# When two column sums, one output tile and one layer's side work are placed later in a slot stream

## The reference

```python
for i in range(DEPTH):                       # DEPTH = 4, kinds 0, 1, 2, 0
    xn = rms_norm(h, norm_gain[i])
    m = diff_attention(...) | mla(...) | rglru_block(...)      # kind = i % 3
    h = h + m
    g = sigmoid(rms_norm(h, ple_norm[i]) @ ple_w_gate[i])
    h = h + g * (p[i] @ ple_w_proj[i])
```

## Time and profile before

| | |
|---|---|
| median of 3 runs | 3595.81 us (3591.43 to 3596.21) |
| the profiled execution | 3592.54 us, its span 3590.7 us |
| TensorE busy | 3481.8 us, 97% of the span |
| VectorE, ScalarE, GpSimd busy | 77%, 55%, 16% |
| mean granted TensorE clock | 0.991 |

### The profile page before, as it was taken

How to read it: one execution, slowest core, us unless ns; L and a number is a source line. 1 busy time by engine, 2 the same in 40 slices (tenths; PEclk the granted TensorE clock), 3 DMA queues, 4 the chain that set the end, 5 groups by cost and what they waited for, 6 DMA issues and landing times.

```text
span 3590.7 us, 68527 instructions
## 1 busy us (share of the span) xinstructions
PE 3481.8 (97%) x27986; PEld 3404.9 (95%) x27986; DVE 2782.3 (77%) x4529; ACT 1981.2 (55%) x3204; POOL 560.6 (16%) x546
## 2 busy tenths in 40 slices
PE   7999999999999999999999999999999999999997
PEld 7999999999999999999999999999999998999997
DVE  7787788677797887877877797888888867666665
ACT  6554546656556686565554446665656646434344
POOL 2111112111113011131111112221212310000000
PEclk9999999999999999999999999999999999999999
DMA  6555556544465444655555475445454444555552
GB/s 240 208 196 214 206 203 240 183 161 167 155 270 193 175 165 176 264 187 211 204 214 200 172 280 186 156 165 212 165 211 165 155 163 148 191 208 183 216 188 106
DMA packets 104905, 691.17 MB, mean 192 GB/s; under 512 B 12688, under 2 KB 21008, under 8 KB 22672
## 3 DMA queue, kind: packets, MB, share of 16 engines
q1 hardware_dynamic: 104128, 685.14, 51.6%
q0 software_dynamic: 464, 1.64, 0.1%
HBM read 676.25 MB, written 2.10 MB: 189 GB/s over the span
## 4 chain that ended last, share of the span: by engine, by line
PE 54%; DVE 9%; ACT 5%; issue 2%; DMA 2%; POOL 1%; SPq 0%; DVEq 0%; POOLq 0%; ACTq 0%
PE g L442 16%; PE g L444 16%; PE g L443 16%; DVE w_lo L1578 3%; ACT w_hi L1034 2%; DMA scratch<-scratch 1%; DMA w_raw<-in_slots 1%; POOL scratch L2386 1%; DVE acc L1643 1%; PE turn_bank L481 1%; PE rope_bank L804 1%; PE out_bank L816 1%; PE norm_bank L455 0%; DVE scratch L1643 0%; DVE h L2202 0%
## 5 line engine op out<-in xcount | busy, mean ns | idle before, releaser
L1578 DVE TENSOR_TENSOR w_lo<-w_raw,w_hi 128x1024 fp32r<-128x1024 f32 x1088 | 1334.5, 1229 | 471.7 <-ACT w_hi L1034 460.1
L1034 ACT ACTIVATE w_hi<-w_raw 128x1024 fp32r<-128x1024 f32 x1088 | 1132.9, 1054 | 998.1 <-PE g L444 865.1
L442 PE MATMUL g<-p_hi,w_hi 128*128 128x256 f32 x4576 | 1322.3, 289 | 36.5 <-DVE w_lo L1578 23.1
L443 PE MATMUL g<-p_lo,w_hi 128*128 128x256 f32 x4576 | 1298.0, 284 | 0.0
L444 PE MATMUL g<-p_hi,w_lo 128*128 128x256 f32 x4576 | 1298.0, 284 | 0.0
L442 PE MATMUL g<-q_hi,w_hi 128*128 128x256 f32 x3408 | 982.3, 288 | 6.1 <-DVE scratch L2281 2.1
L444 PE MATMUL g<-q_hi,w_lo 128*128 128x256 f32 x3408 | 965.4, 283 | 0.0
L443 PE MATMUL g<-q_lo,w_hi 128*128 128x256 f32 x3408 | 965.3, 283 | 0.0
L442 PEld LDWEIGHTS g<-p_hi,w_hi 128*128 128x128 f32 x4576 | 881.0, 193 | 53.5 <-DVE w_lo L1578 33.6
L443 PEld LDWEIGHTS g<-p_lo,w_hi 128*128 128x128 f32 x4576 | 881.1, 193 | 1.4
L444 PEld LDWEIGHTS g<-p_hi,w_lo 128*128 128x128 f32 x4576 | 880.8, 192 | 0.0
(11 more groups left out here) (451 smaller groups left out, 3973.4 us busy)
## 6 DMA issues: line engine op xcount, KB each, us to landing
w_raw<-in_slots SPq DMA_DIRECT2D x640, 1024.0 KB, 4.9
scratch<-scratch SPq DMA_DIRECT2D x128, 64.0 KB, 4.9
h<-in_x SPq DMA_DIRECT2D x4, 512.0 KB, 6.1
out_h<-h SPq DMA_DIRECT2D x4, 512.0 KB, 2.6
sq<-in_p POOLq DMA_DIRECT2D x4, 256.0 KB, 3.0
con<-in_consts SPq DMA_DIRECT2D x1, 832.0 KB, 10.6
scratch<-in_distance POOLq DMA_DIRECT2D x1, 576.0 KB, 5.5
vec<-in_vecs SPq DMA_DIRECT2D x1, 383.0 KB, 3.8
```

What stands on the lines that cost most here:

```text
L442: pe.matmul(g, wh, hi[:, k], start=n == 0, stop=False)
L443: pe.matmul(g, wh, lo[:, k], start=False, stop=False)
L1034: act.activation(w_hi[k % SPLIT][:, cols], raw[MAIN_AT[k] % RAW][:, cols], ACT.Copy).then_inc(hi_ready, 1)
L1578: dve.tensor_tensor(w_lo[k % SPLIT][:, cols], raw[MAIN_AT[k] % RAW][:, cols], w_hi[k % SPLIT][:, cols], SUB).then_inc(lo_ready, 1)
```

## The change

It moves work, and adds and removes none:

1. The column sum of a head is closed behind the head's second tile (j == 1) in place of the first; the last one of layers 0 and 3 behind output tile 2 in place of the middle of the projection. The reading side on VectorE moves with it.
2. For the last output tile of each layer, ScalarE and VectorE first finish the tile (add, high part, square, low part) and then split the slot two further on, first half and second.
3. In the recurrence layer VectorE does `begin`, `take`, `lo_half(1)` first, in every slot, and `c_gates`, `c_split` and `low` behind them; and the z values lie in three buffers, the third being `acc`.

```diff
--- before.py
+++ after.py
@@ -335,7 +335,7 @@
     xbp = rsn.rearrange("p a b -> p (a b)")[:, 0:528].rearrange("p (a b) -> p a b", a=2)
     rg = view(DT * SEQ, 4, SEQ)
     ig = view(20 * SEQ, 4, SEQ)
-    c_gz, c_zc = view(24 * SEQ, 2, SEQ), [cos_b[:], sin_b[:]]
+    c_gz, c_zc = [view(24 * SEQ, SEQ), view(25 * SEQ, SEQ), acc[:]], [cos_b[:], sin_b[:]]
     soft = view(25 * SEQ, 3, DT)
     c_half = tiny[:, 20:21]
     group_banks = (bR, bT, bO, bN)
@@ -584,6 +584,8 @@
         def out_and_gates(layer, y, x, begun):
             for n in range(begun, DT):
                 square_tiles(*y, arriving=DT if n == 0 else 0)
+                if n == 2 and layer in (0, 3):
+                    mod_columns([acc[:]])
                 if n in (5, 9, 13):
                     mod_columns(ple_acc)
             gates(layer, *x)
@@ -639,7 +641,7 @@
                         pe.matmul(bS[s][:, 0:P], q[:, 0:P], k[:, 0:P], start=True, stop=True)
                         pe.matmul(bS[s][:, P:3 * P], q[:, P:SEQ], k, start=True, stop=True).then_inc(scored, 1)
                     c.next("score_read", 2)
-                if j == 0 and prev:
+                if j == 1 and prev:
                     mod_columns([acc[:]])
 
         def layer_a(layer, x, y):
@@ -651,7 +653,6 @@
             w, s = slot(), c.k["slot"]
             pe.wait_ge(factor_ready, c.at("norm"))
             proj_half(layer, 0, w, range(4), s)
-            mod_columns([acc[:]])
             out_0 = begin_out()
             pe.wait_ge(x_lo, c.at("x", A_HEADS - 1))
             part(out_0, *y, 0, 4)
@@ -1117,8 +1118,15 @@
             act.wait_ge(p_ready, c.at("p"))
             for i in range(0, 4):
                 for j in range(4):
-                    tick()
-                    tail(i * 4 + j, x[0], vec[:, bass.ds(i * 4 + (a + j), 1)], tile_taken, c.at("tile"), j % 2)
+                    n = i * 4 + j
+                    if n < DT - 1:
+                        tick()
+                        tail(n, x[0], vec[:, a + n:a + n + 1], tile_taken, c.at("tile"), j % 2)
+            c.next("slot")
+            tail(DT - 1, x[0], vec[:, a + DT - 1:a + DT], tile_taken, c.next("tile"), 1)
+            act.wait_ge(half_used, c.next("half"))
+            hi_ahead(0)
+            hi_ahead(1)
             factor(rstd[:], bank=bT)
             gates(y[0], VEC["norm_gain"] + (layer + 1) * DT, layer == DEPTH - 1)
 
@@ -1305,7 +1313,7 @@
 
             def y_high(n):
                 act.wait_ge(gated, c.next("gated"))
-                act.activation(y[0][:, n], c_gz[:, n % 2], ACT.Copy).then_inc(x_hi, 1)
+                act.activation(y[0][:, n], c_gz[n % 3], ACT.Copy).then_inc(x_hi, 1)
             for s, (kind, n) in enumerate(C_ORDER):
                 c.next("slot")
                 act.wait_ge(half_used, c.next("half"))
@@ -1695,12 +1703,19 @@
             for i in range(0, 4):
                 for j in range(4):
                     n = i * 4 + j
-                    begin()
-                    g = take(columns=n in (6, 10, 14) or (n, layer) in ((0, 0), (1, 1), (0, 3)))
+                    if n < DT - 1:
+                        begin()
+                    else:
+                        c.next("slot")
+                    g = take(columns=n in (6, 10, 14) or (n, layer) in ((3, 0), (1, 1), (3, 3)))
                     dve.tensor_tensor(h[:, n], g, h[:, n], ADD).then_inc(tile_taken, 1)
-                    lo_half(1)
+                    if n < DT - 1:
+                        lo_half(1)
                     dve.wait_ge(tile_taken, c.at("tile"))
-                    tail(n, x, vec[:, bass.ds(i * 4 + (a + j), 1)])
+                    tail(n, x, vec[:, a + n:a + n + 1])
+                    if n == DT - 1:
+                        lo_half(0)
+                        lo_half(1)
                     ada_half(ple_acc, j % 2)
             factor()
             gates(layer, y, VEC["norm_gain"] + (layer + 1) * DT, layer == DEPTH - 1)
@@ -1746,7 +1761,7 @@
                     a_silu(1)
                     a_weigh(jl)
                 begin()
-                g = take(columns=j == 1 and prev)
+                g = take(columns=j == 2 and prev)
                 if first and j == 0:
                     factor()
                 dve.wait_ge(scaled, c.at("scaled"))
@@ -1991,7 +2006,7 @@
 
         def layer_c(layer, x, y):
             lam_ = vec[:, VEC["c_lambda"]:VEC["c_lambda"] + DT]
-            z = c_gz[:, 0, 0:DT]
+            z = c_gz[0][:, 0:DT]
             link(dve.tensor_scalar(z, lam_, -1.0, None, MUL))
             softplus(z, soft[:, 0], soft[:, 1], soft[:, 2], sp8, sp8)
             link(dve.tensor_scalar(sp8, sp8, 8.0, None, MUL))
@@ -2008,17 +2023,20 @@
 
             def finish(n):
                 dve.wait_ge(sig_ready, c.next("sig"))
-                link(dve.tensor_tensor(c_gz[:, n % 2], c_gz[:, n % 2], c_zc[n % 2], MUL))
-                dve.tensor_tensor(c_gz[:, n % 2], c_gz[:, n % 2], xc[:, n], MUL).then_inc(gated, 1)
+                link(dve.tensor_tensor(c_gz[n % 3], c_gz[n % 3], c_zc[n % 2], MUL))
+                dve.tensor_tensor(c_gz[n % 3], c_gz[n % 3], xc[:, n], MUL).then_inc(gated, 1)
 
             def low(n):
                 dve.wait_ge(x_hi, c.next("x"))
-                dve.tensor_tensor(y[1][:, n], c_gz[:, n % 2], y[0][:, n], SUB).then_inc(x_lo, 1)
+                dve.tensor_tensor(y[1][:, n], c_gz[n % 3], y[0][:, n], SUB).then_inc(x_lo, 1)
                 dve.wait_ge(x_lo, c.at("x"))
             for s, (kind, n) in enumerate(C_ORDER):
-                if kind == "z" and n > 1:
-                    low(n - 2)
                 begin()
+                if kind == "in":
+                    dve.tensor_tensor(xbp[:, n % 2, 3:259], take(), rstd[:], MUL).then_inc(tile_taken, 1)
+                if kind == "z":
+                    dve.tensor_tensor(c_gz[n % 3], take(), rstd[:], MUL).then_inc(tile_taken, 1)
+                lo_half(1)
                 for g in range(4):
                     if s == C_AT[g] + 1:
                         c_gates(g)
@@ -2026,14 +2044,11 @@
                         dve.wait_ge(conv_done, 4 * g + 4)
                         c_split(g)
                 if kind == "in":
-                    dve.tensor_tensor(xbp[:, n % 2, 3:259], take(), rstd[:], MUL).then_inc(tile_taken, 1)
-                if kind == "z":
-                    dve.tensor_tensor(c_gz[:, n % 2], take(), rstd[:], MUL).then_inc(tile_taken, 1)
-                lo_half(1)
-                if kind == "in":
                     conv(n)
                 if kind == "z" and n:
                     finish(n - 1)
+                if kind == "z" and n > 1:
+                    low(n - 2)
                 if kind == "z" and n == 12:
                     split_p(layer)
                 for g in range(4):
@@ -2470,7 +2485,7 @@
                 if kind != "group":
                     c.next("tile")
                 if kind == "z":
-                    clamp(c_zc[n % 2], c_gz[:, n % 2])
+                    clamp(c_zc[n % 2], c_gz[n % 3])
             out_and_gates(layer)
```

## The result

The changed kernel takes 3566.01 us, median of 4 runs (3563.81 to 3569.41), against 3593.62 us for the kernel before in the same comparison: a ratio of 0.9927, 95% interval 0.9909 to 0.9944. It is faster, and the forecast was 3566. The profiled execution took 3567.6 us, with a span of 3565.8, where the sum of the prediction had put it at 3563.0; how that fits the median is told at the end.

The account below looks back on a forecast made before the run. TensorE, busy 3481.8 of 3590.7 us, was taken as the bound, with only waits and clock to recover. 3592.5 - 38.5 + 9 = 3563.0 us for the profiled execution, median 3566, range 3556 to 3576.

Parts of the forecast that it names:

- signs of being wrong: Slots 12 to 35 of the recurrence layer getting shorter, or norms or scores in the heads waiting 1 us or more.
- column sums in the heads, with their clock: Heads of layers 0 and 3: 14 waits for `acc` go, net 17.1 us, plus 5.1 us of low clock.
- the last sum, with its clock: Projections of layers 0 and 3: 7.9 us of waits and 6.7 us of half clock saved, 14.6 us.
- the last output tile: Layers 0 and 3: waits worth 3.0 us go, later `w_lo` returns 0.5 and 0.8; net 1.7 us.
- recurrence layer: Slots 12 to 35: 5.7 us of waits plus 3.4 of low clock, rounded 9 us slower.
- old wait less about 1.4: Head norms behind the second tile: wait by this rule, 0.7 us in two heads, nothing in most.
- two stretches of 6.7 us give 6.7: Both projections: two 6.7 us stretches at half clock end, giving 6.7 us.
- two stretches, 3.4 us: Recurrence layer: longer waits add two stretches at half clock, costing 3.4 us.
- The first: Rival: ScalarE's lag is absorbed and the recurrence layer gains 8 us; 3549 us; chance 0.15.
- The second: Rival: heads wait again at norm or scores, a third of 17.1 us stays; 3581 us; chance 0.14.
- The third: Rival: all 16 waits for `acc` reappear one tile later; about 3596 us; chance 0.04.
- the fourth: Rival: longer waits keep the recurrence layer's clock low, making the kernel slower; decides at 3603 us; chance 0.03.

Follow-up runs that it names:

- heads_only: Kernel before with only the column sums of heads 1 to 7 of layers 0 and 3 closed one tile later: 3574.86 us, ratio 0.9950.
- tail_only: Kernel before with only the last output tile of each layer finished first: 3593.53 us, ratio 0.9998.
- recurrence_only: Kernel before with only the new order of the recurrence layer and its three z buffers: 3600.26 us, ratio 1.0021.
- split_early: Changed kernel with the split of the group's input ahead of the take again, gate evictions still behind: 3564.47 us, ratio 0.9921.
- last_sum_only: Kernel before with only the last column sum of layers 0 and 3 moved from the projection to output tile 2: 3577.20 us, ratio 0.9961.
- old_recurrence: Changed kernel with the recurrence layer as before, with two z buffers and gates, split and low parts ahead of the take: 3558.52 us, ratio 0.9904.

## Why the prediction came out as it did

The direction, the place of every gain and the sign of the recurrence layer were right. One of the prediction's own signs of being wrong did appear: a norm in the heads waited by more than 1 us (1.77). By its own steps, with changes of the profiled execution in us:

| step | predicted | measured |
|---|---|---|
| column sums in the heads, with their clock | -22.2 | -18.3 (-21.4 in `heads_only`) |
| the last sum, with its clock | -14.6 | -13.2 |
| the last output tile | -1.7 | -2.3 (-1.5 in `tail_only`) |
| recurrence layer | +9 | +8.2 (7.6, and 0.6 ahead of slot 12) |
| all other places | 0 | +0.6 |
| sum | -29.5 | -24.9 |

**Heads.** The mechanism held: all 14 waits are gone and no low stretch is left in the heads. The norm waits were forecast for the two heads with old waits of 2.1 us, 0.7 each; they are there with 0.63 each. Three more came: 0.9 and 0.6, and the 1.8 behind the long issue; by the rule "old wait less about 1.4" none of these three should wait for more than 0.1 us. `heads_only`, without the last, is within 1 us of the forecast by its windows. In that agreement there is luck: 5.1 us of the forecast are the three low stretches of one execution. The four profiles of kernels with the old head waits have 3, 2, 1 and 1, which at 1.7 us each is 3.0 us on average.

**Last sum.** The waits were priced rightly, the clock too high: I took half of 6.7 us twice. But the earlier trace rows shows TensorE busy for only 5.06 and 5.80 of those 6.70 us, and at half clock only busy time is lost: 2.5 + 2.9 = 5.4. With it the term is 7.9 + 5.4 = 13.3, and 13.2 was measured. The step that failed is the term "two stretches of 6.7 us give 6.7".

**Last output tile.** The return of 0.5 us for `w_lo` came in layer 3 (0.49) and not in layer 0, where TensorE found it ready.

**Recurrence layer.** The chain was right at its beginning and at its ends, and the sum nearly, but the split into waits and clock was not. Forecast were 5.7 us of waits and 3.4 of clock. The layer rows give 15.4 us idle now against 13.6, 1.8 more, and 5.8 us more of busy time: of clock, since five more stretches of 3.4 us ran at the lower level, not two. (TensorE is busy for 18.8 us in the low stretches, half of which is 9.4, against 1.7 before; that is even more than 5.8, and fewer waits, with the 0.16 us that the prediction puts to each, give some back.) The two prices are not independent. A slower TensorE arrives later at the next wait and finds it shorter: the waits of 0.5 and 1.0 us that I had put behind the one of 2.7 did not appear, and the products behind it ran at half clock for 3.4 us, which is 1.7 us of delay. That the one hid the other is argued from these sizes. The step that failed here is the term "two stretches, 3.4 us".

**The total.** The sum of the prediction was 4.6 us too good for the profiled execution (rounded: 3.9 in the heads, 1.4 in the last sum, 0.6 elsewhere, less 0.6 in the last tile and 0.8 in the recurrence layer). That the median is met to 0.1 us is luck: the profiled execution of the changed kernel lay 1.6 us over its median, while that of before, by which the sum was set, lay 3.3 under its own. The gain by medians is 27.6 us.

**Rivals.** The first (the recurrence layer gains) is refuted by `recurrence_only`. The second (heads give back) happened to the extent of 3.9 us, most of it by a transfer and not by VectorE's load. Its time had a slip: the three low stretches that it keeps are 5.1 us by the prediction's own price, not 3.4, so it stood for 3583 us, not 3581. The third is refuted by the waits view, which has no wait for a column sum left. The clock did fall in the recurrence layer and rose again each time, so the fourth never came near.

## What to carry to other kernels

Where one engine must wait for a reduction that another finishes late, move the consumer behind the next piece of independent work, and look what is late next: here that was worth some 33 us of waits and clock. "Free the bank first" is no rule by itself: side work that feeds another engine's critical input has the same claim, and being 1.6 us late with the gates cost 5.7 us in a layer that already had no slack (the late split another 2.4, in the profile alone). When a change has several parts, measure them apart even when the whole is faster: here one of three lost 8 of the others' 34, and leaving it out, or using its third buffer to move the sigmoid, gives 3558 or 3554 us.

## What was not expected of the hardware

In the recurrence layer of the changed kernel each of the five waits of 1.9 to 3.1 us came with a stretch of 3.4 or 6.8 us at a granted clock of 0.50, but this does not hold from one execution to the next. At the boundary of a head in layer 0 a wait of 2.08 us was followed by the lower level in the kernel before (351.26) and one of 2.07 was not in `tail_only` (350.83). In `split_early` a wait of 2.46 us (1344.78) was followed by full clock. At the first boundary one of 1.52 us was followed by the lower level, and one of 1.32 was not (`last_sum_only`, 80.9 us).

This shows in the spread of the times. The kernel before ran from 3585.17 to 3601.64 us in 17 runs, and `tail_only`, which keeps all the head waits, from 3585.36 to 3600.38 in 12. Kernels without head waits and without the projection wait stayed within 1.4 us (`old_recurrence`, 4 runs) to 5.6 us (the changed kernel, 4 runs), though so few runs also show less of a range. The clock goes with it: among the 17 runs the two fastest (3585.17 and 3588.66) had a mean granted clock of 0.993, and the two slowest (3601.60 and 3601.64) one of 0.990. By an estimate from these numbers, 0.003 of 3590 us is 10.8 us, most of the 15 between them.

And the issue of a small transfer of 64 KB on SyncE took 0.60 us in most cases and 1.4 to 2.6 in some kernels at the same place, enough to hold VectorE for 2.7 us.
